# The Down stage of a decoder's feed-forward parts in seven block products, with differences of weights on GpSimd and VectorE

## The reference, cut to what matters

```python
def swiglu(x, w_gu, w_down):
    g, u = jnp.split(x @ w_gu, 2, axis=-1)
    return (jax.nn.silu(g) * u) @ w_down

f = swiglu(rmsnorm(h, g[N_FFN1_PRE]), ffn_w_gu[layer, 0], ffn_w_down[layer, 0])
h = h + 0.5 * rmsnorm(f, g[N_FFN1_POST])
```

## Time and profile before

| | |
|---|---|
| median of 3 runs | 2197.55 us (2197.55 to 2197.93) |
| profiled execution: span from the first to the last instruction | 2196.3 us |
| what lies around the span, to the median | 1.25 us |
| PE busy | 2181.2 us |
| granted PE clock, mean | 0.999 |

### The profile page before, as it was taken

One profiled execution on the slowest core, in us unless ns is written; L12 is line 12 of the kernel. 1 busy time (PEld: TensorE's weight loads), 2 busy tenths in 40 slices (PEclk: granted clock), 3 DMA queues, 4 the chain that ended last, 5 costly groups with the idle time before them and its releaser, 6 DMA issues.

```text
span 2196.3 us, 36637 instructions
## 1 busy us (share of the span) xinstructions
PE 2181.2 (99%) x13844; PEld 1944.0 (89%) x13844; DVE 1456.1 (66%) x2185; ACT 1127.0 (51%) x1881; POOL 110.4 (5%) x104
## 2 busy tenths in 40 slices
PE   9999999999999999999999999999999999999999
PEld 8999888775888899998899998887868889999987
DVE  8888636788666598874388885345266656888732
ACT  6555524476554565563365554245345546555531
POOL 0000000675000000000000000000000000000000
PEclk9999999999999999999999999999999999999999
DMA  4332332221452233332323323322214422333322
GB/s 164 105 105 95 115 106 63 77 77 49 144 165 79 74 115 105 105 105 96 115 87 105 105 95 115 115 81 87 96 36 138 155 79 77 103 105 105 110 99 78
DMA packets 61953, 221.44 MB, mean 101 GB/s; under 512 B 7953, under 2 KB 8081, under 8 KB 61858
## 3 DMA queue, kind: packets, MB, share of 16 engines
q1 hardware_dynamic: 57456, 208.69, 28.9%
q10 hardware_dynamic: 4402, 11.46, 1.5%
HBM read 218.03 MB, written 2.10 MB: 100 GB/s over the span
## 4 chain that ended last, share of the span: by engine, by line
PE 93%; DVE 4%; ACT 1%; POOL 1%; issue 1%; DMA 0%; DVEq 0%; POOLq 0%
PE ps L2099 12%; PE ps L2100 12%; PE ps L2101 12%; PE ps L2195 11%; PE ps L2197 11%; PE ps L2196 11%; PE ps L479 6%; PE ps L480 6%; PE ps L481 6%; PE ps L2035 1%; DVE e_sc L1768 1%; DVE e_max L1767 1%; DVE e_sc L1783 1%; PE ps L2583 0%; PE ps L2560 0%
## 5 line engine op out<-in xcount | busy, mean ns | idle before, releaser
L417 DVE TENSOR_TENSOR w_lo<-w_raw,w_hi 128x1024 fp32r<-128x1024 f32 x204 | 252.5, 1241 | 358.2 <-ACT w_hi L412 357.3
L412 ACT ACTIVATE w_hi<-w_raw 128x1024 fp32r<-128x1024 f32 x210 | 221.6, 1057 | 311.4 <-PE ps L2197 225.4
L2099 PE MATMUL ps<-t_hi,w_hi 128*128 128x256 f32 x1280 | 362.3, 283 | 0.0
L2100 PE MATMUL ps<-t_lo,w_hi 128*128 128x256 f32 x1280 | 362.2, 283 | 0.0
L2101 PE MATMUL ps<-t_hi,w_lo 128*128 128x256 f32 x1280 | 362.2, 283 | 0.0
L2099 PE MATMUL ps<-x_hi,w_hi 128*128 128x256 f32 x960 | 271.7, 283 | 0.0
L2100 PE MATMUL ps<-x_lo,w_hi 128*128 128x256 f32 x960 | 271.7, 283 | 0.0
L2101 PE MATMUL ps<-x_hi,w_lo 128*128 128x256 f32 x960 | 271.7, 283 | 0.0
L1490 DVE TENSOR_TENSOR w_lo<-f,w_hi 128x1024 fp32r<-128x1024 f32 x152 | 186.2, 1225 | 124.0 <-ACT w_hi L840 124.0
L479 PE MATMUL ps<-x_hi,w_hi 128*128 128x256 f32 (+1 forms) x736 | 250.8, 341 | 1.6 <-DVE x_lo L1367 0.9
L480 PE MATMUL ps<-x_lo,w_hi 128*128 128x256 f32 (+1 forms) x736 | 246.0, 334 | 0.0
(11 more groups left out here) (352 smaller groups left out, 4317.8 us busy)
## 6 DMA issues: line engine op xcount, KB each, us to landing
w_raw<-in_wstream SPq DMA_DIRECT2D x310, 512.0 KB, 3.3
w_raw_odd<-in_wstream SPq DMA_DIRECT2D x80, 512.0 KB, 3.3
tmp<-in_post_gains ACTq DMA_DIRECT2D x8, 512.0 KB, 5.1
gain_bc<-in_gains ACTq DMA_DIRECT2D x7, 512.0 KB, 3.8
h<-in_x SPq DMA_DIRECT2D x4, 512.0 KB, 5.7
c_mem<-in_mem ACTq DMA_DIRECT2D x2, 1024.0 KB, 5.8
out_dram<-h SPq DMA_DIRECT2D x3, 512.0 KB, 2.7
c_gain<-in_mem_gains ACTq DMA_DIRECT2D x2, 512.0 KB, 7.5
```

Of the source, the lines that this page charges most:

```text
L412: nc.scalar.activation(weights(v)[0], raw(v), ACT.Copy).then_inc(w_hi_ready, 1)
L417: nc.vector.tensor_tensor(wl, raw(v), wh.bitcast(f32), ALU.subtract).then_inc(w_ready, 1)
L2099: nc.tensor.matmul(dst, wh[:, at], xh[:, b, :], start=first, stop=False, skip_group_check=True)
L2100: nc.tensor.matmul(dst, wh[:, at], xl[:, b, :], start=False, stop=False, skip_group_check=True)
```

## The change: what it does

The Down product of 512 tokens x 2816 by 2816 x 1024 is cut into blocks: two halves of the tokens; the 22 row blocks of 128 into the even and the odd ones, 11 each (`QT`); two halves of the columns. Seven products of blocks (`LOW_2`, `LOW_1`, `SUM_1`, `SUM_2`, `LOW_3`, `SUM_3`, `SUM_4`, in this order) stand in place of eight. Each has 11 row blocks in six units (`PU`): five of two row blocks (128 x 1024) and one of one (128 x 512), for two token tiles. So there are 42 units, with 66 matmuls of 512 columns in each product.

- Four products have a difference of weight blocks as a factor, one per unit. Of the six units of each, DVE forms two (`SUMS_V`, units 1 and 4) and POOL four.
- Three have a sum or difference of operand blocks, which POOL forms (`first`, `second`, `third`); a fourth such (`s3_sum`) POOL forms during gate_up, tile by tile.
- Operand halves are made per unit (2 x 256 columns) by ACT (`op_upper`) and DVE (`op_lower`) into a ring of nine places.
- Partial sums that two outputs share are copied from PSUM to `f` by ACT (`keep_tiles`), and DVE adds the other part from PSUM (`down_add`). ACT squares from `f`; POOL multiplies the first two tiles by the gain (`gained`), DVE the others.
- Post, update and the next part's norm of tiles 0 and 1 now stand inside the stage; those of tiles 2 and 3 after it. The last two units are taken tile by tile, with the next part's first two turns between them.
- SP has six more raw places, for `LOW_1`. Raw blocks are loaded again where a difference needs them: 42 loads a stage (35 of 512 KB, 7 of 256 KB) in place of 22.

The diff, cut to its core:

```diff
-    "ffn": [("gate_up", 2 * FT), ("down", FT)],
+    "ffn": [("gate_up", 2 * FT), ("down", PRODUCTS * PU)],
...
         def split_hi(act, v):
-            act.wait_ge(w_in[RAW[v]], RAW_COUNT[v] * 16)
+            if v in DOWN and DOWN[v][1] in SUMMED:
+                act.wait_ge(down_sum_v if DOWN[v][2] in SUMS_V else down_sum, sum_count(v))
+            else:
+                act.wait_ge(w_in[RAW[v]], RAW_COUNT[v] * 16)
...
+            def ffn(i):
+                n0, s0, d0 = nffn[i] * FT, SEVENS[i], U[i, "down"]
+                q0 = 3 * PU * nffn[i]
+                for k in range(QT):
+                    pool.wait_ge(gu_free, n0 + 2 * k + 3)
+                    place = by_half[:, 0, 1, k, :]
+                    nc.gpsimd.tensor_tensor(place, by_half[:, 0, 0, k, :], place, ALU.subtract).then_inc(s3_sum, 1)
...
+                def block_sum(p, m):
+                    v = d0 + PU * p + m
+                    if m in SUMS_V:
+                        return
+                    pool.wait_ge(w_in[RAW[v]], RAW_COUNT[v] * 16)
+                    if p == SUM_3:
+                        pool.wait_ge(down_sum, sum_count(d0 + PU * SUM_2 + m))
+                        nc.gpsimd.tensor_tensor(raw(v), block_place(m), raw(v), ALU.subtract).then_inc(down_sum, 1)
...
+                def gained(o):
+                    pool.wait_ge(o_sq, square_count(i, o, 1))
+                    pool.wait_ge(post_in, 16 * (i + 1))
...
+                pool.wait_ge(prod, 5 * (s0 + FT))
+                for m in range(PU):
+                    second(m)
+                    first(m)
+                for m in range(PU):
+                    block_sum(SUM_1, m)
+                for m in range(PU):
+                    block_sum(SUM_2, m)
+                for m in range(PU):
+                    third(m)
+                gained(0)
+                for m in range(PU):
+                    block_sum(SUM_3, m)
+                gained(1)
+                for m in range(PU):
+                    block_sum(SUM_4, m)
...
+            def op_lower(i, c):
+                dve.wait_ge(op_hi, nffn[i] * PRODUCTS * PU + c + 1)
+                hi, lo = operand_place(c)
+                nc.vector.tensor_tensor(lo, operand(c // PU, c % PU), hi.bitcast(f32), ALU.subtract)\
+                    .then_inc(op_ready, 1)
...
+            def down(i):
+                d0, last = U[i, "down"], PRODUCTS * PU
+                ahead = 4
+                for c in range(last):
+                    if d0 + c + AHEAD < NU:
+                        split_lo(dve, d0 + c + AHEAD)
+                    p, m = divmod(c + AHEAD + 1, PU)
+                    if p in SUMMED and m in SUMS_V:
+                        block_sum(i, p, m)
+                    while ahead <= min(c + 6, 2 * c + 5, last - 1):
+                        op_lower(i, ahead)
+                        ahead += 1
...
+                    if c == PU * SUM_4:
+                        down_add(i, 0, 2)
+                        down_add(i, 0, 3)
+                        post(i + 1, 0)
+                        update(i + 1, 0)
...
+                        if c in (last - 4, last - 3):
+                            norm_scale(i + 1, c - (last - 4))
+                        if c >= last - 2:
+                            norm_lower(i + 1, c - (last - 2))
...
+                def tiles(c, t, final):
+                    p, m = divmod(c, PU)
+                    pe.wait_ge(w_ready, d0 + c + 1)
+                    pe.wait_ge(op_ready, PRODUCTS * PU * nffn[i] + c + 1)
...
+                for a in range(2):
+                    if i + 1 < NP:
+                        turn_x(i + 1, a)
+                    for c in (PRODUCTS * PU - 2, PRODUCTS * PU - 1):
+                        last = tiles(c, (a,), c == PRODUCTS * PU - 1)
```

More of the change, by code:

```diff
@@ L32 @@
 SEVEN = FT - PLAIN
+QT = FT // 2
+PU = -(-QT // 2)
+PRODUCTS = 7
+LOW_2, LOW_1, SUM_1, SUM_2, LOW_3, SUM_3, SUM_4 = range(PRODUCTS)
+BLOCK = (1, 0, 2, 3, 3, 0, 1)
+RING = 9
 PARTS = [("ffn", 0, 0), ("even", 0, 0), ("cross", 0, 0), ("ffn", 0, 1),
@@ L673, in _ @@
                     gla(i)
+                elif parts[i][0] == "ffn":
+                    ffn(i)
         @block.scalar
@@ L787, in norm @@
                     whole(1)
+                    whole(2)
+                    upper(3)
+                    whole(3)
+                elif parts[i - 1][0] == "ffn":
+                    down_square(i - 1, 1, 2)
+                    post_mean(i, 2)
+                    down_square(i - 1, 1, 3)
+                    post_mean(i, 3)
+                    whole(0)
+                    square(2)
+                    whole(1, (0,))
+                    square(3)
+                    whole(1, (1,))
+                    upper(2)
                     whole(2)
@@ new lines, in ffn, with op_upper @@
+                down(i)
+            def op_upper(i, c):
+                p, m = divmod(c, PU)
+                if p == LOW_2:
+                    act.wait_ge(gu_free, nffn[i] * FT + 2 * (2 * m + TILES[m] - 1) + 4)
+                elif p in (SUM_1, SUM_2, LOW_3):
+                    done = {SUM_1: 2 * m + 2, SUM_2: 2 * m + 1, LOW_3: 2 * PU + m + 1}[p]
+                    act.wait_ge(op_sum, 3 * PU * nffn[i] + done)
+                elif p == SUM_3:
+                    act.wait_ge(s3_sum, QT * nffn[i] + 2 * m + TILES[m])
+                if c >= RING:
+                    act.wait_ge(w_free, U[i, "down"] + c - RING + 3)
+                nc.scalar.activation(list(operand_place(c))[0], operand(p, m), ACT.Copy).then_inc(op_hi, 1)
@@ L1415, in norm @@
                     return lower
+                elif parts[i - 1][0] == "ffn":
+                    down_add(i - 1, 1, 2)
+                    down_add(i - 1, 1, 3)
+                    post(i, 2)
+                    update(i, 2)
+                    post(i, 3)
+                    update(i, 3)
+                    scale(2)
+                    scale(3)
+                    lower(2)
+                    lower(3)
                 else:
```

440 lines of the change are left out of this document (335 added, 105 removed).

## The result

The changed kernel takes **2318.64 us** (median of four runs, 2318.36 to 2319.33) against 2197.55 (four runs, 2197.43 to 2197.93): a ratio of 1.055 with a 95% interval from 1.0536 to 1.0566. That is 121 us slower, where 84 were forecast: the right case, at the far end of its range.

What follows compares the result with a forecast made beforehand. PE bounds the kernel before; after the change DVE and POOL, taking turns, would bound the Down stages. 3 x 20.6 + 17.3 + 3 + 1.5 = 83.6 us on 2197.55 gave 2281 us, range 2230 to 2330.

Steps and rivals of the forecast that it cites:

- the right case: Down stages: PE busy well under 80%, 1024-column operations lengthened (DVE above 2 us, POOL above 3), stage about 142 us.
- Turns: Down stages: DVE's two-SBUF-source operations and POOL's arithmetic alternate, so their times add: 130.4 us where PE needs 104.9; chance 0.81.
- handover chain: Down stages: if PE waits while DVE and POOL are both idle, handovers were the bound, not turns; no size given.
- the signs that were to show it: Down stages: PE well under 80% busy, DVE's 1024 columns above 2 us, POOL's above 3, stage about 142 us.
- the sum for one stage, in turns: Down stage: DVE 73.7, POOL 56.7, other costs 6, tail 5.9: 142.3 us against 121.7, +20.6.
- Rival 3: Down stages: turns, and TensorE's clock falls because PE starves; +50 us, 2330 us in all; chance 0.05.
- 3 x 20.6 and 17.3: Time added in the four Down stages: 20.6 us in each of three, 17.3 in the last.
- high end: 2330 us: 15 us of gaps, POOL at its lone 1.29, gate_up and SP bounds in part; +33 a stage.
- Around the stage: Outside the Down stages: gate_up 0 (at most 6.6), SP 0 (at most 3), part changes +1 each, end +1.5 us.
- Rival 1: Down stages: DVE and POOL run side by side, PE is the bound, a stage takes 106.7 us, kernel 2142; chance 0.11.

Runs made afterwards that it cites:

- run 4: Changed kernel with all six weight differences of each product on DVE, none on POOL: 2284.49 us, ratio 1.0396 to the kernel before.
- memset run: Changed kernel with POOL's feed-forward arithmetic replaced by three memsets of the same destination each, waits and signals kept: 2206.16 us, ratio 1.004.
- run 8: Changed kernel with PE's turns, DVE's norm scales and the halves of the next part's x reordered at the change of parts: 2319.21 us, ratio 1.0551.
- run 5: Changed kernel with POOL's two-operand feed-forward operations made one-operand (times 1 plus 0), waits and signals kept: 2189.98 us, ratio 0.9963.

## Why the prediction was right, and where its sum fell short

**Turns: right.** The mechanism is the one forecast, DVE's two-source operations and POOL's arithmetic one after the other. Three runs show it: POOL that only writes (minus 27 us in the stage), POOL with one operand (minus 31), POOL left out (minus 18 although DVE has more to do). The first keeps POOL as late as it was and every handover in place, and so excludes a handover chain as the main bound. Handovers are a smaller second cost, by run 4.

Of the signs that were to show it, the lengthened operations came as forecast only where the engines meet: about 2.3 us for a low there, but 1.63 in the mean, and 2.85 to 2.96 for POOL's 1024 columns where above 3 was said. PE was busy 81% of the stage and not well under 80, because its matmuls took 121 us where 106.7 were counted, at the clock of 0.90.

**The sum of a stage: 142.3 forecast, 150.1 measured in the second.** The step that failed is "the sum for one stage, in turns", in its sizes. Up to the end of the norm scale (1014.2 to 1156.4) it said 73.7 of DVE, 56.7 of POOL and 6 for adds, statistics and idle time, 136.4 us; measured were 142.2. The memset run gives DVE's part without turns: 86.5 us busy up to the same scale (983.5 to 1098.0). DVE or POOL was busy in 137.7 us of those 142.2, so POOL added 51.2, and 4.5 were idle.

- DVE was **mis-sized by some 9 us**: 86.5 against 73.7 and the six adds of 0.6. I took the gaps 1.08 and 0.54 from a list of turns, where each operation of DVE follows one of POOL. Most of this stage's follow another of DVE, or end before a wait, and then they cost more: a low of 1024 columns is followed after 1.13 us and one of 512 after 0.60, as DVE's timeline at the end of the second stage shows, with POOL idle:

```profile
1150.44 0.68 DVE L489 TENSOR_TENSOR w_late_d<-d_t,w_late_d 128x512 fp32r<-128x512 f32 x1
1151.04 0.16 DVE L1606 RECIPROCAL stat<-stat 128x1 f32<-128x1 f32 x1
...
1152.44 1.22 DVE L489 TENSOR_TENSOR w_lo<-w_raw,w_hi 128x1024 fp32r<-128x1024 f32 x1
1153.57 0.16 DVE L1588 TENSOR_SCALAR stat<-stat 128x2 f32<-128x2 f32 x1
```

  Counted to the next operation's start, or to its own end before a wait, an operation of the memset run costs 1.14 us for 1024 columns, 0.64 for 512 and 0.41 for 256, where 1.08, 0.54 and 0.30 were taken: over 90 operations some 7 us. The rest is 1.2 us of small statistics and 0.7 for two products of gate_up's end.
- POOL was forecast 5.5 us too dear, 56.7 against 51.2. Beside DVE's operations that read PSUM POOL is not held up, which the sum left out; how much of the 5.5 that makes, no run shows.
- Idle time and tail were 2 us short each. After the scale 7.9 us pass, not 5.9, for the turns and the 18 matmuls left over run partly at the lower clock. PE had just stood still for 8.0 us, and the granted clock of the stretch behind that is 0.75:

```profile
1156.40:1164.26 7.86, 7.83 (x34) 6.64 (x35) 6.85 (x9) 4.06 (x6) 0.00 (x0) 0.75 0.45 136
```

  PE's timeline has the first of these matmuls 0.42 us apart, where 0.227 was worked out from the earlier trace rows:

```profile
1159.06 0.63 PE L2529 MATMUL ps<-w_late_d,d_op 128*128 128x512 f32 x1
1159.48 0.63 PE L2527 MATMUL ps<-w_late_d,d_op 128*128 128x512 f32 x1
```

  Rival 3 was thus partly true: the clock fell to 0.90 in the stages. On the path it shows as these 2 us in a stage and not as 50 in the whole. Up to the scale DVE or POOL was busy in all but 4.5 us and PE stood still for 28.9, so there a faster PE would mostly have waited longer; no run tests that by itself.

The gaps weigh on all four stages. In place of 3 x 20.6 and 17.3 there are 31.1 (240.2 to 393.3 against 239.5 to 361.5), 28.4, 29.4 and 20.8: 109.7 instead of 79.1, the largest part of the error. The range held the result, but not by the terms that its high end was made of: it had 15 us of idle time, a dearer POOL, and something for gate_up and SP, where the second stage had 4.5 us idle, a cheaper POOL and more of DVE. That the sum of those terms reached as far as 2318.6 is partly luck.

**Around the stage.** The three changes of parts cost 7.3 us instead of 3, the end 2.7 instead of 1.5. At the second of the three changes one sees why: PE waits another 1.6 us in the next part's first 17 (above, run 8), so DVE's queue is still behind when that part begins. POOL's differences in gate_up were priced at 0.6 us and took 1.6 each (44 in all). They were covered as forecast, but for at most the 0.7 us by which the first stage begins later. SP moved 138 GB/s in the stage; whatever its loads held up lies within the 5.5 us in which both DVE and POOL were idle.

**Rival 1 was priced wrong, which the result alone would not show.** It gave 2142 us for work side by side. The memset run is close to that case (POOL's memsets are busy 70.7 us a stage where the forecast had 57), and it takes 2206, not faster than before. Its second stage lasts 122.7 us where 106.7 were counted. PE stood still for 11.0 of the 16 us between, 6.2 of them waiting for the norm scale at the end, and its matmuls took 5 us longer, at a clock of 0.96. In the fourth stage, which has no next part behind it, the same run needs 114.7 us against 119.9 before. Only with POOL's time cut as well (run 5) does the time fall below the kernel before, by 8 us. So even with little or nothing lost to turns the seven products gain next to nothing here. The rival compared an engine's busy time with the bound and left out the end of the stage, where DVE has the next part's scales to make while PE has 18 matmuls left.

## What to carry to other kernels

- Before work is shared between VectorE and GpSimd, look for two operations of them at the same time in a trace, and list their ends. If they alternate, the sum counts and not the longer of the two; here the whole work on VectorE alone was 74 us faster than shared out.
- Price an operation by its lone spacing, and add the other engine's turn where the two meet. Durations in a contended stretch hold both, and the gaps between the ends there (1.08 and 0.54) were shorter than the lone spacing (1.13 and 0.60).
- A pause of PE at the end of a stage was worth nothing while the engine that feeds it was full on both sides of that pause: three edits of the order there changed the time by less than 1 us.

## What the runs showed of the hardware that was not expected

- GpSimd's one-operand arithmetic (a multiply and an add with constants) takes turns too, but a short one: a DVE operation beside 1024 columns of it lasted some 0.85 us longer (1.53 instead of 0.68), and the GpSimd operation itself 1.40 us in the mean, against 2.85 to 2.96 with two operands. It stretched DVE's stage by 14%, two operands by 42%.
- GpSimd's memsets cost VectorE's two-operand subtractions nothing: 1.223 us for a low beside them, 1.225 without. One operation of another kind that fell beside them, a tensor_scalar of 128x2, lasted 0.99 us instead of 0.16 and ended with the memset.
- An 8-column operation of GpSimd lasts 1.11 us in the median beside a busy VectorE and 0.20 beside an idle one. What it pays is the other's turn.
